# Three-layer decoder block in split fp32: a new order in layer 1, a fused distance pass, and an earlier start

## The reference, cut to what matters

```python
memn = rms_norm(mem, mem_norm_w)
for layer in range(2):                      # layer 0: retention, layer 1: differential attention
    u = rms_norm(x, attn_norm_w[layer]) @ w_in[layer]
    ...
    q = rms_norm(q, diff_q_norm_w[j])       # 6 heads x 2 maps x 64
    k = rms_norm(k, diff_k_norm_w[j])
    o = rms_norm(diff_attention(q, k, v, lam), diff_subln_w[j]) * (1.0 - lambda_init)
    qc = rms_norm(u[..., 3 * MAIN_WIDTH:], mem_q_norm_w[layer])
    mkv = memn @ w_mem_kv[layer]            # 4 heads of memory attention
    x = x + concatenate([o, o_mem]) @ w_out[layer]
    gu = rms_norm(x, ffn_norm_w[layer]) @ w_gate_up[layer]
    x = x + (silu(gu[..., :FFN]) * gu[..., FFN:]) @ w_down[layer]

def diff_attention(q, k, v, lam):           # for one head
    sc = q_c @ k_c.T * d ** -0.5            # two maps, c = 0, 1
    sc = where(chunk(j) <= chunk(i), sc - slope[h] * abs(i - j), -inf)
    p = softmax(sc)
    return (p[0] - lam * p[1]) @ v
```

## Time and profile before

| | us |
|---|---|
| runs shown (3) | 1116.76, 1123.24, 1123.5; median 1123.24 |
| profiled execution | 1124.99 |
| its span, first to last instruction | 1123.2 |
| mean granted TensorE clock | 0.982 |

### The profile page before, as it was taken

How to read it: one execution, slowest core, us unless ns; L and a number is a source line. 1 busy time by engine, 2 the same in 40 slices (tenths; PEclk the granted TensorE clock), 3 DMA queues, 4 the chain that set the end, 5 groups by cost and what they waited for, 6 DMA issues and landing times.

```text
span 1123.2 us, 24024 instructions
## 1 busy us (share of the span) xinstructions
PE 1069.1 (95%) x8706; PEld 1028.5 (92%) x8706; DVE 767.4 (68%) x1323; ACT 591.9 (53%) x1063; POOL 172.4 (15%) x186
## 2 busy tenths in 40 slices
PE   6999999999999879799999999989999999999999
PEld 5989999999999778689999999989788999999998
DVE  5865686666556876775666557867777669999843
ACT  6654564444544544464444545655455556666532
POOL 3100121111110001031111110001111014444400
PEclk9999999999999998989999999999899999999999
DMA  7533455555665222335555665443232255555563
GB/s 264 183 122 108 130 177 181 183 187 172 184 188 169 95 85 83 115 128 181 181 184 177 184 183 168 159 144 121 88 112 87 85 207 172 185 187 180 156 214 106
DMA packets 50904, 174.45 MB, mean 155 GB/s; under 512 B 5648, under 2 KB 6928, under 8 KB 50704
## 3 DMA queue, kind: packets, MB, share of 16 engines
q1 hardware_dynamic: 50832, 173.46, 47.4%
HBM read 172.39 MB, written 1.05 MB: 154 GB/s over the span
## 4 chain that ended last, share of the span: by engine, by line
PE 81%; DVE 13%; ACT 3%; issue 2%; POOL 1%; DMA 1%; SPq 0%; DVEq 0%; ACTq 0%; POOLq 0%
PE bank L640 24%; PE bank L641 24%; PE bank L642 24%; DVE ring_lo L1384 3%; DVE xw_lo L1390 1%; PE bank L729 1%; DVE tmp L1501 1%; PE bank L820 1%; PE bank L853 1%; PE bank L743 1%; PE bank L840 1%; ACT tmp L1148 1%; PE bank L800 1%; PE bank L918 1%; DVE negmax L1624 1%
## 5 line engine op out<-in xcount | busy, mean ns | idle before, releaser
L640 PE MATMUL bank<-xw_hi,ring_hi 128*128 128x256 f32 x1736 | 499.8, 288 | 3.7 <-ACT lam L1284 1.1
L641 PE MATMUL bank<-xw_lo,ring_hi 128*128 128x256 f32 x1736 | 492.0, 283 | 0.0
L642 PE MATMUL bank<-xw_hi,ring_lo 128*128 128x256 f32 x1736 | 491.8, 283 | 0.0
L1384 DVE TENSOR_TENSOR ring_lo<-ring_raw,ring_hi 128x1024 fp32r<-128x1024 f32 (+1 forms) x336 | 400.1, 1194 | 55.2 <-ACT ring_hi L972 49.5
L972 ACT ACTIVATE ring_hi<-ring_raw 128x1024 fp32r<-128x1024 f32 (+1 forms) x336 | 340.8, 1017 | 92.2 <-PE bank L642 84.5
L640 PEld LDWEIGHTS bank<-xw_hi,ring_hi 128*128 128x128 f32 x1736 | 333.9, 192 | 11.8 <-issue 6.2
L641 PEld LDWEIGHTS bank<-xw_lo,ring_hi 128*128 128x128 f32 x1736 | 334.0, 192 | 0.2
L642 PEld LDWEIGHTS bank<-xw_hi,ring_lo 128*128 128x128 f32 x1736 | 333.7, 192 | 0.0
L640 PE MATMUL bank<-act_hi,ring_hi 128*128 128x256 f32 x784 | 228.0, 291 | 14.8 <-DVE ring_lo L1764 8.8
L641 PE MATMUL bank<-act_lo,ring_hi 128*128 128x256 f32 x784 | 225.1, 287 | 0.0
L642 PE MATMUL bank<-act_hi,ring_lo 128*128 128x256 f32 x784 | 225.0, 287 | 0.0
(11 more groups left out here) (175 smaller groups left out, 918.6 us busy)
## 6 DMA issues: line engine op xcount, KB each, us to landing
ring_raw<-w_up SPq DMA_DIRECT2D x132, 512.0 KB, 3.2
ring_raw<-w_in SPq DMA_DIRECT2D x85, 512.0 KB, 3.3
ring_raw<-w_down SPq DMA_DIRECT2D x48, 512.0 KB, 3.6
ring_raw<-w_down SPq DMA_DIRECT2D x24, 384.0 KB, 3.9
ring_raw<-w_oa SPq DMA_DIRECT2D x16, 384.0 KB, 3.0
ring_raw<-w_kv SPq DMA_DIRECT2D x8, 512.0 KB, 6.6
ring_raw<-w_ob SPq DMA_DIRECT2D x8, 512.0 KB, 3.3
ring_raw<-w_oa SPq DMA_DIRECT2D x8, 512.0 KB, 3.6
```

The lines of the kernel that those rows point to most:

```text
L640: mm(bank[b][:, 0:T], w_hi, tile(hi, t), start=kk == 0, stop=False)
L641: mm(bank[b][:, 0:T], w_hi, tile(lo, t), start=False, stop=False)
L642: last = mm(bank[b][:, 0:T], w_lo, tile(hi, t), start=False, stop=end)
L1384: V.tensor_tensor(ring_lo[:, a:b], ring_raw[:, a:b], ring_hi[:, a:b].bitcast(f32), SUB).then_inc(lo_done, 1)
```

## The change

1. `in1` comes in another order (all of the queries and keys of heads 0 to 3 ahead of values 12 and 13), and nearly every step of layer 1 gets another slot. No slot holds a `norm` and `scores`. `softmax` is the first step of its slot.
2. `oa1` covers four mixed tiles (6, 7, 0, 1; 256 KB a load) and `ob1` the other four (2 to 5; four loads, two outputs a load).
3. The norms of layer 1 alternate between PSUM banks 4 and 7.
4. ScalarE writes six distance tables, one for each head's slope (`slopes`, slots 2 to 7), where layer 0's decay tables stood. Queries are scaled by a negative factor, so the scores are negated; one VectorE instruction for each block (128 and 256 columns) adds the table and takes the minimum. The exponential takes scale -1.
5. Both maps' reciprocals are one instruction.
6. At the start only the stream weights of the parameters are loaded first, the first kv tile in two loads, each with its own semaphore; squares come later; the other parameters are loaded and scaled after the first tiles.

```diff
-          ("in1", 20, [8], 20), ("oa1", 8, [6], 8), ("ob1", 2, [8], 2), ("up1", 44, [8], 4), ...
+          ("in1", 20, [8], 20), ("oa1", 8, [4], 8), ("ob1", 4, [8], 4), ("up1", 44, [8], 4), ...
-              "oa1": [6, 7, 0, 1, 2, 3], "ob1": [4, 5],
+              "oa1": [6, 7, 0, 1], "ob1": [2, 3, 4, 5],
-         "in1": [18, 19] + [t for j in range(3) for t in (2*j, 2*j+1, 6+2*j, 7+2*j, 12+2*j, 13+2*j)],
+         "in1": [18, 19, 0, 1, 6, 7, 2, 3, 8, 9, 12, 13, 4, 5, 10, 11, 14, 15, 16, 17],
...
-    norm(1, 2, 18)
-    norm(1, 4, 0)
-    norm(1, 6, 6)
+    for t, slot in ((18, 2), (0, 3), (6, 5), (2, 7), (8, 9), (4, 13), (10, 15), (8 + 64, 20)):
+        norm(1, slot, t)
+    norm(1, 16, 6 + 64, True)
+    norm(1, 23, 10 + 64, True)
     mem_pairs(1)
-    for n, slot in enumerate((7, 8, 13, 14, 19, 20)):
+    for h in range(DIFF_HEADS):
+        at(1, 2 + h, "slopes", h)
+    for n, slot in enumerate((11, 12, 17, 18, 19, 20)):
         at(1, slot, "turn", 12 + n)
-    for h, slot in enumerate((9, 10, 14, 15, 22, 23)):
-        unit(1, slot, "diff", h, 2)
-    (norms 2, 8, 70, 4, 72, 10, 74 from slots 9, 11, 13, 15, 17, 19, 25;
-     mixes 6, 7 in slot 11, 0, 1 in 16, 2, 3 in 19, 4, 5 in 27)
+    for h, slots in enumerate(((9, 10, 11, 12), (11, 12, 13, 14), (13, 14, 15, 18), (15, 16, 17, 19),
+                               (18, 19, 20, 21), (20, 21, 21, 22))):
+        first, soft, turned, last = slots
+        at(1, last, "values", "diff", h)
+        for m in range(2):
+            plan[1][soft].insert(0, ("softmax", "diff", h, 1 - m))
+        at(1, turned, "weights", "diff", h)
+    for h, slot in enumerate((9, 11, 13, 15, 18, 20)):
+        for m in range(2):
+            at(1, slot, "scores", "diff", h, m)
+    for k, slot in ((6, 11), (7, 11), (0, 19), (1, 19), (2, 23), (3, 23), (4, 26), (5, 26)):
+        at(1, slot, "mix", k)
...
+        def norm_bank(n):
+            ...
+            return bank[7 if 0 <= n - first < count_ and (n - first) % 2 else 4]
...
-            sp.dma_start(par[:, :], params_in).then_inc(par_loaded, 16)
+            streams = PCOL["memq0"]
+            sp.dma_start(par[:, 0:streams], params_in[:, 0:streams]).then_inc(weights_loaded, 16)
...
-            load_kv(0)
+            half = DM // 2
+            sp.dma_start(ring_raw[:, 0:half], w["kv"][ds(0, P), 0:half]).then_inc(half_loaded, 16)
+            sp.dma_start(ring_raw[:, half:DM], w["kv"][ds(0, P), half:DM]).then_inc(w_loaded[0], 16)
             for n in range(1, 4):
                 load_mem(n)
             load_kv(1)
+            sp.dma_start(par[:, streams:NPARAM], params_in[:, streams:NPARAM]).then_inc(par_loaded, 16)
...
                 pe.wait_ge(np_sq, number["squares", (layer, t)] + 1)
-                bank4_free()
+                if layer != 1:
+                    bank4_free()
+                elif n >= 2:
+                    pe.wait_ge(np_out, n - 1)
...
+            def slopes(layer, h):
+                act.wait_ge(r_pt, RET_HEADS)
+                A(u[:, DECAY + h * 384:DECAY + (h + 1) * 384], cmat("dist", 384), ACT.Copy,
+                  scale=SLOPE[h]).then_inc(sloped, 1)
...
                     last = A(p[:, a:a + width], src[:, a:a + width], ACT.Exp, bias=negmax[:, c:c + 1],
-                             accum_out=rowsum[:, c:c + 1])
+                             scale=1.0 if kind == "mem" else -1.0, accum_out=rowsum[:, c:c + 1])
...
             for m in range(2):
                 stream_hi(0, m, u)
-            for m in range(2):
-                stream_square(0, m, u)
-            act.wait_ge(w_loaded[0], 16)
-            for half, done in ((0, first_hi), (1, hi_done)):
+            for half, loaded, done in ((0, half_loaded, first_hi), (1, w_loaded[0], hi_done)):
+                act.wait_ge(loaded, 16)
                 a = half * DM // 2
                 A(ring_hi[:, a:a + DM // 2], ring_raw[:, a:a + DM // 2], ACT.Copy).then_inc(done, 1)
             for m in range(2, KT):
                 act.wait_ge(mem_loaded[m // 2], 16)
                 stream_hi(0, m, u)
-                if m > 2:
-                    stream_square(0, m - 1, u)
-            stream_square(0, KT - 1, u)
+                if m >= 6:
+                    stream_square(0, m - 6, u)
             for g in range(1, AHEAD):
                 split_hi(PH["kv"], 0, g - AHEAD)
+                for m in range(3 * g - 1, 3 * g + 2):
+                    stream_square(0, m, u)
+            act.wait_ge(par_loaded, 16)
...
-                V.scalar_tensor_tensor(s[:, 0:384], cmat("dist", 384), -SLOPE[h], b[:, 0:384], MUL, ADD).then_inc(sm_b, 2)
-                dve.wait_ge(sm_b, 2 * number["biased", (layer, kind, h, m)] + 2)
+                dve.wait_ge(sloped, h + 1)
                 for it, (a, width) in enumerate([(0, P), (P, T)]):
-                    last = V.tensor_reduce(negmax[:, c + it:c + it + 1], s[:, a:a + width], AX, ALU.max, negate=True)
+                    far = DECAY + h * 384 + a
+                    last = V.tensor_tensor_reduce(s[:, a:a + width], b[:, a:a + width], u[:, far:far + width], 1.0, 3e38,
+                                                  ADD, ALU.min, negmax[:, c + it:c + it + 1])
...
-                small_op(V.reciprocal(rrow[:, c:c + 2], rowsum[:, c:c + 2]))
+                if kind == "diff" and m == 0:
+                    return
+                if kind == "diff":
+                    small_op(V.reciprocal(rrow[:, :], rowsum[:, :]))
+                else:
+                    small_op(V.reciprocal(rrow[:, c:c + 2], rowsum[:, c:c + 2]))
```

More of the change, by code:

```diff
@@ L42 @@
           ("in0", 20, [8], 20), ("oa0", 8, [6], 8), ("ob0", 2, [8], 2), ("up0", 44, [8], 4), ("down0", 24, [8, 8, 6], 12),
[1 row of a table removed]
[1 row of a table added]
           ("in2", 45, [8], 45), ("oa2", 16, [8, 4], 16), ("ob2", 4, [8], 4), ("up2", 44, [8], 4), ("down2", 24, [8, 8, 6], 12)]
-OUT_INPUTS = {"oa0": [6, 7, 0, 1, 2, 3], "ob0": [4, 5], "oa1": [6, 7, 0, 1, 2, 3], "ob1": [4, 5],
+OUT_INPUTS = {"oa0": [6, 7, 0, 1, 2, 3], "ob0": [4, 5], "oa1": [6, 7, 0, 1], "ob1": [2, 3, 4, 5],
               "oa2": list(range(12)), "ob2": list(range(12, 16))}
@@ L501, in roots_of @@
             return normed(n)[:, 0:P]
+        def norm_bank(n):
+            first = min(number["norm", k] for _, k in number if type(k[0]) is str and k[1] == 1 and _ == "norm")
+            count_ = sum(1 for _, k in number if type(k[0]) is str and k[1] == 1 and _ == "norm")
+            return bank[7 if 0 <= n - first < count_ and (n - first) % 2 else 4]
         def norm_no(layer, t):
@@ L715, in norm @@
                 pe.wait_ge(np_sq, number["squares", (layer, t)] + 1)
-                bank4_free()
+                if layer != 1:
+                    bank4_free()
+                elif n >= 2:
+                    pe.wait_ge(np_out, n - 1)
+                if (layer, t) == (1, 0):
+                    pe.wait_ge(rstd_done, 4)
                 if (layer, t) == (2, 20):
@@ L719, in norm @@
                 for d in range(4):
-                    last = mm(bank[4][32 * d:32 * d + 32, 0:P], cmat(SPEC[layer, t][0], 32),
+                    last = mm(norm_bank(n)[32 * d:32 * d + 32, 0:P], cmat(SPEC[layer, t][0], 32),
                               normed(n)[:, d * P:(d + 1) * P], start=True, stop=True)
@@ L728, in spread @@
                 for d in range(4):
-                    last = mm(bank[4][:, d * P:(d + 1) * P], spread_r[:, d * P:(d + 1) * P], root_parts[:, :],
+                    last = mm(norm_bank(n)[:, d * P:(d + 1) * P], spread_r[:, d * P:(d + 1) * P], root_parts[:, :],
                               start=True, stop=True)
@@ L1103, in roots @@
                 act.wait_ge(np_ms, n + 1)
-                A(y, bank[4][:, 0:width], ACT.Ln, scale=scale, bias=eps(e)).then_inc(np_ln, 1)
+                A(y, norm_bank(n)[:, 0:width], ACT.Ln, scale=scale, bias=eps(e)).then_inc(np_ln, 1)
                 act.wait_ge(np_ln, n + 1)
@@ L1236, in ssd_square @@
                 A(gsq if t % 4 else gsum, tile(u, 8 + t), ACT.Square).then_inc(gs_sq, 1)
-            DO = {"squares": squares, "norm": norm, "group_norm": group_norm, "turn": turn, "decays": decays,
+            DO = {"squares": squares, "norm": norm, "group_norm": group_norm, "turn": turn, "decays": decays, "slopes": slopes,
                   "ret_out": ret_out, "gate_silu": gate_silu, "scores": scores, "weights": weights, "mix": mix,
@@ L1549, in newton_step @@
                 dve.wait_ge(np_rt, n + 1)
-                v = bank[4][:, 0:y.shape[1]]
+                v = norm_bank(n)[:, 0:y.shape[1]]
                 V.scalar_tensor_tensor(v, v, eps(0), y, ADD, MUL).then_inc(np_nt, 1)
@@ L1562, in norm @@
                 dve.wait_ge(np_nt, 5 * n + 3)
+                if number["stat", (layer, t)]:
+                    dve.wait_ge(np_bc, number["stat", (layer, t)])
                 V.tensor_copy(root_hi[:, :], y).then_inc(np_nt, 1)
@@ L1574, in norm_out @@
```

(7 more changed lines are left out.)

30 lines of the change are left out of this document (6 added, 24 removed), and 2 rows, old and new, of the table PHASES.

## The result

The changed kernel takes 1108.18 us (median of 4 runs, 1107.22 to 1109.17) against 1122.01 for the kernel before, measured beside it (4 runs): ratio 0.9874, 95% interval 0.9831 to 0.9916. 1109.5 was predicted. Two repeats (e1, e12) gave 0.9863 (0.9833 to 0.9893) and 0.9863 (0.9837 to 0.9890). So a sum of stages by the two profiles comes out up to 3.9 us too high.

A forecast was written before the change was run, and what follows sets the result against it. TensorE, busy 95% of the span, was taken as the bound, so time comes from its idle and slow stretches. Startup 3.8, waits 6.5, clock 2.5 and handover 1.0 sum to 13.8 us: about 1109.5 us, range 1101 to 1118.5.

The forecast's parts named there:

- startup: First kv tiles: PE starts sooner and tile 1 is split sooner; 3.8 us gained at the mean-square matmul (bounds 1.5 and 5).
- fused pass: Layer 1's softmax: VectorE takes 0.8 us a map for 1.11; 0.3 us a head shows, 1.8 us of the waits gained.
- order: Layer 1's mixing part: norms and scores in separate slots; PE's waits 11.3 us for 17.8, gain 6.5 including the fused pass.
- clock: Layer 1's mixing part: fewer PE waits over 2 us leave 5.5 of 8 us lost to low clock, gain 2.5.
- handover: From ob1 to up1: at 1.45 us an output VectorE nearly keeps up, so the first up1 tile drags less; 1.0 us.
- the squares finish on GpSimd at about 16.1, so the mean-square matmul is not late: Startup: the sums of squares are ready by 16.1 us, so PE's mean-square matmul behind kv tile 1 needn't wait.
- Rival 2: Startup is set by the loads; only half a microsecond to 1.6 is left of its gain: 1112, chance 0.08.
- only the first map's saving lies on a head's path, 0.3 us: Layer 1's heads: the second map queues behind ScalarE's exponentials, so a head's path falls from 6.4 to 6.1 us.
- Rival 4: Slower: the fused pass needs several cycles an element, delaying heads and next roots; 1130 at 3.5 us a map, chance 0.05.
- Slots 0 to 8: Start of layer 1's plan comes out even: a 0.8 us wait for a turn goes, 0.7 for spread 6 comes.
- Rival 1: Layer 1's waits only move: 17.8 us and the clock stay, only startup and handover remain; 1118.5, chance 0.18.
- Rival 3: The new order hides nearly all: under 4 us of waits in layer 1 and no low clock; 1097, chance 0.09.

The follow-up runs named there:

- e1: The changed kernel timed again as a yardstick, nothing altered: 1107.57 us (6 runs), ratio 0.9863 to the kernel before.
- e12: The changed kernel timed once more as a yardstick, nothing altered: 1108.41 us, ratio 0.9863 to the kernel before.
- e8: First mean-square matmul behind the third kv tile instead of the second, on the changed kernel: 1107.28 us, where the changed kernel took 1107.57.
- e10: Five of the eight first squares between the high parts instead of two, on the changed kernel: 1105.73 us, changed kernel beside it 1108.41.
- e2: Fused pass undone (an add, then two maxima, no slope tables) on the changed kernel: 1113.05 us, 5.5 us slower than the changed kernel.
- e9: Changed kernel without the fused pass and the new start, leaving the new order, split output projection, second bank and one reciprocal: 1112.38 us, before 1123.74.
- e11: Early squares and layer 1's norm roots ahead of the weight tile's low part, together on the changed kernel: 1104.32 us, 4.1 us below the changed kernel.
- e7: Output projection split into four and four mixed tiles alone, on the kernel before with its plan unchanged: 1122.65 us, ratio 0.9994.
- e3: New start undone (parameters in one load, first kv tile in one load, squares between high parts) on the changed kernel: 1108.76 us, 1.2 us slower, not resolved.

## Why the prediction was right

The sum was 13.8 us and 13.8 were measured between the medians (15.4 and 15.3 in the repeats). The direction, the main cause (waits of PE in layer 1) and the size hold. That the two numbers agree to a tenth is luck: startup was put too high, and the fused pass and the order too low.

| term | predicted | measured |
|---|---|---|
| startup | 3.8 | 1.7 to the first mean-square matmul; 1.2 and 2.5 by the times, neither resolved |
| order: waits without the fused pass's share, clock, handover | 4.7 + 2.5 + 1.0 = 8.2 | 11.4 by the times, 10.0 of layer 1 |
| fused pass | 1.8 | 4.0 and 5.5 by the times, 5.9 and 4.2 of layer 1 |

- **Startup: failed at "the squares finish on GpSimd at about 16.1, so the mean-square matmul is not late".** They finished at 18.9. Up to tile 1 every time was within 0.4 us (7.2 and 7.6, 13.1 and 13.2). But I priced GpSimd's adds at 0.75 us each, and six took 6.64 us; in the kernel before, six took 5.38. Four of the six took 0.72 to 0.74 us, with about 0.14 us between two. The other two took 1.47 and 1.52: each began while VectorE was subtracting for the low part of a kv tile (11.92 to 13.15 and 15.17 to 16.59) and ended 0.6 us behind it. ScalarE also waits for them (squares 4 and 7 waited 1.3 us each), so the chain runs alternately through both. e8 and e10 fit this: asking later gained nothing, and summing earlier took the wait of PE away, though its worth is not resolved by the times. Rival 2, that the loads bind, fell: tile 1's split followed ScalarE's queue and PE had it at 13.2. That its 0.5 to 1.6 us comes near what was left is chance.
- **Fused pass: failed at its size.** 0.8 us a map was taken and 0.6 was the low end; it is 0.56. The accumulator reads that the Trainium skill speaks of ("VectorE: DVE Perf Modes", section "Two Vector instructions with no wait between them") are there, 24 of them, so the rule holds. But one takes 83 ns and overlaps the next pass, not ScalarE's 187, and the main pass takes 289 and 420 ns, less than the rows I took it from (351 and 478). And "only the first map's saving lies on a head's path, 0.3 us" gave too little. The path fell by about 1 us: the first exponential starts 0.68 us behind VectorE's first pass for 1.22, and the second map's 0.90 us behind the first's for 1.11, since before it was VectorE's pace that held them and not ScalarE's 1.0 us a map. The next roots follow the softmax (e2). Rival 4 (slow pass) is out; its 1130 was also added up wrongly: at 12 us for each us a map above 1.1, less the 13.8 gained, 3.5 us a map gives 1138.
- **Order: mechanism right, the sum of the waits a little smaller.** Predicted and measured, in order: spread 8 1.65, 0.75; slot 11's weights 0.4, 0.52; spread 4 1.3, 0.74; spread 10 2.7, 1.75; slot 17's weights 0.4, 0.78; mixes 0 and 1 0.6, 1.0; slot 20's weights 0.4, 0.52; head 5 2.2, 1.71; spread 72 0.6, 0; spread 74 1.0, 0.91; and 1.04 at the start of ob1, where none was expected. Sum 11.3 and 9.7. Much of the difference is the fused pass: without it (e9) spreads 8, 4 and 10 wait 1.61, 2.53 and 2.34 us.
- **Slots 0 to 8: not even, but 1.6 us better.** The two old waits of 0.86 and 0.78 went and the one for spread 6 didn't come.
- **Clock:** 4.7 us by what is left of layer 1's 15.6 after 9.8 of waits and 1.1 of handover, for 2.5 predicted. It is a remainder between two single profiles, and such a stage differs by 2 us from one profile to another, so the two numbers can hardly be told apart. The handover was right (1.0).
- **Rival 1** (the waits only move) fell for the whole change: 19.5 us of waits became 9.7. Rival 3 needed under 4 us of waits; with e11 the kernel is still at 1104.

Undoing the fused pass costs 5.5 us and adding it alone gains 4.0, and the parts alone sum to 17.9 against 13.8 to 15.4 together; with intervals 4 to 6 us wide on each, no more can be said about whether they add. What the order, the split, the second bank and the one reciprocal are worth singly is open but for the split (e7).

## What to carry to other kernels

Lay in-order engines out slot by slot, and follow a saving past its own chain: on a queue that serves heads and norms in turn, whatever comes earlier moves all that stands behind it. Give a step and what waits for it (here softmax and the transposes behind it) a slot between them: the new order, which did this among other things, was worth 11 us, and the waits for a softmax fell from 7.7 to 1.3 us. Keeping steps whose chains cross on a second engine (roots and exponentials on ScalarE) apart was part of the same order, but no run has it alone, and the waits for roots didn't fall with it. When work is pushed back to start a tile sooner, price the slowest reader of what was pushed back, with the durations that it shows beside the work it will then run beside.

## What the runs showed of the hardware

- The same instructions took 128.7 to 128.8 us in four profiles of layer 1 (changed kernel three times, e8) and 126.50 in two (e3, e10). The waits for roots are 4.1 or 4.2 us in the four and 4.7 in the two, the others alike; the difference is the grant. Changed kernel, then e3:

```profile
358.00:490.00 132.00, 122.03 (x972) 110.47 (x972) 102.94 (x249) 76.00 (x176) 18.59 (x18) 0.96 0.36 118
410.00:427.00 17.00, 13.73 (x108) 12.02 (x107) 12.23 (x36) 7.58 (x20) 0.00 (x0) 0.91 0.23 63
```

```profile
358.00:490.00 132.00, 121.49 (x991) 109.85 (x991) 104.20 (x250) 76.85 (x178) 18.72 (x19) 0.99 0.37 121
410.00:427.00 17.00, 13.73 (x120) 12.01 (x119) 12.51 (x38) 7.59 (x20) 0.00 (x0) 1.00 0.23 63
```

The same wait of 1.8 us (1.75 before 421.08 and 1.76 before 421.17) lies in both stretches from 410 to 427 us, and is followed by the low clock in one only. So differences of 2 us between single profiles of one such stage say nothing of the code.
- A fused add and minimum over fp32 in PSUM and SBUF takes 289 ns for 128 columns and 420 for 256, where a plain two-tensor pass with one input in PSUM takes 300 (L1572) and 420 (L1553), and reads its accumulator in 83 ns, which overlaps the next pass.
- GpSimd's 256-column fp32 add took from 723 to 1532 ns in the first 30 us of the changed kernel, with a median of 743. Four of the 14 were slow (1.47 to 1.53 us, begun at 12.27, 15.65, 23.83 and 27.25), and each had begun while VectorE was making the low part of a weight tile, a subtraction of two 128 x 1024 tensors in SBUF (in all four cases the pass had started 0.3 to 0.8 us earlier). It is the same in e10 (1.52 and 1.53 us, begun at 13.09 and 14.75, beside passes from 12.62 to 14.02 and from 14.37 to 15.69). No run takes that pass away, so the cause is not shown.
